# A fused two-block transformer kernel on one core: five changes to the order and the buffers of its stages, the last of them the place of each mLSTM head's step

## What is computed

```python
# first block
n = rmsnorm(h, g_mix);  q_a..z_m = split(n @ w_in)          # 7168 columns
y_a = moba_attention(...)   # 8 heads of 64; y_r = retention(...)  # 4 heads of 128
y_m = memory_attention(q_m, rmsnorm(mem, g_mem), w_mem_kv)  # 4 heads of 128
h = h + (sum of sigmoid(z) * (y @ w_br)) @ w_out
h = h + conv_ffn(rmsnorm(h, g_ffn), w_up, conv_w, conv_b, w_down)   # D_FF = 2816
x = rmsnorm(h, g_final)
# second block, layer 1: mLSTM (4 heads of 256) beside a pooling branch
#   weights of a head: P = (q k^T) * decays;  h = (P v) / max(|sum of P's row|, floor)
#   the head is normed, joined with a skip term and gated by silu(z)
#   pooling branch: windows of 2, 4, 8, 16 tokens, a 256 x 256 matrix for each group
x = x + [ya, yb] @ a_w_out
# second block, layer 2: latent attention (MLA), 8 heads, causal by blocks, output gated
x = x + (attention * silu(z)) @ c_w_out
```

## Time and profile before

| | |
|---|---|
| median of 3 runs | 833.51 us (832.02 to 834.57) |
| the profiled execution | 831.42 us, of which the span from the first to the last instruction is 829.6 us |
| PE busy | 801.0 us, 97% of the span |
| DVE busy | 567.7 us, 68% |
| ACT busy | 432.3 us, 52% |
| POOL busy | 131.4 us, 16% |
| mean granted clock of PE | 0.988 of full |

### The profile page before, as it was taken

One profiled execution on the slowest core, in us unless ns is written; L12 is line 12 of the kernel. 1 busy time (PEld: TensorE's weight loads), 2 busy tenths in 40 slices (PEclk: granted clock), 3 DMA queues, 4 the chain that ended last, 5 costly groups with the idle time before them and its releaser, 6 DMA issues.

```text
span 829.6 us, 11993 instructions
## 1 busy us (share of the span) xinstructions
PE 801.0 (97%) x4640; PEld 698.8 (84%) x4640; DVE 567.7 (68%) x938; ACT 432.3 (52%) x585; POOL 131.4 (16%) x98
## 2 busy tenths in 40 slices
PE   8799999999999999999999999999999989998998
PEld 7588788888888899999988888998898868876766
DVE  5555566796468677878764495769864895896763
ACT  5745544344534475655643464645745245795441
POOL 0011650000000005454440000041410000042000
PEclk9899999999999999999999999999999999998999
DMA  9887433325455465554545544334655333743101
GB/s 342 323 286 258 152 124 134 142 109 172 145 191 203 168 245 192 200 171 186 196 162 201 202 153 170 135 127 167 231 183 190 107 109 115 283 162 143 51 1 51
DMA packets 23220, 142.78 MB, mean 172 GB/s; under 512 B 3548, under 2 KB 4456, under 8 KB 7040
## 3 DMA queue, kind: packets, MB, share of 16 engines
q1 hardware_dynamic: 20016, 134.51, 45.2%
q10 hardware_dynamic: 1776, 4.12, 1.3%
q0 software_dynamic: 1376, 3.43, 1.2%
HBM read 140.97 MB, written 2.64 MB: 173 GB/s over the span
## 4 chain that ended last, share of the span: by engine, by line
PE 77%; DVE 14%; ACT 4%; issue 2%; DMA 2%; SPq 0%; ACTq 0%; DVEq 0%
PE gemm L471 15%; PE gemm L472 15%; PE gemm L473 15%; PE gemm L477 8%; PE gemm L478 8%; PE gemm L479 8%; DVE wlo L1646 4%; DMA raw<-in_weights 2%; ACT whi L1148 2%; DVE xc L2165 2%; PE head L537 1%; PE head L727 1%; PE head L872 1%; PE head L871 1%; DVE rs_a L1656 1%
## 5 line engine op out<-in xcount | busy, mean ns | idle before, releaser
L1646 DVE TENSOR_TENSOR wlo<-raw,whi 128x2048 fp32r<-128x2048 f32 x122 | 282.1, 2314 | 119.9 <-ACT whi L1148 119.7
L1148 ACT CAST whi<-raw 128x2048 fp32r<-128x2048 f32 x122 | 232.6, 1906 | 216.9 <-PE gemm L473 122.3
L471 PE MATMUL gemm<-whi,x0hi 128*128 128x512 f32 (+2 forms) x400 | 158.7, 397 | 4.3 <-DVE x0lo L1833 2.6
L473 PE MATMUL gemm<-whi,x0lo 128*128 128x512 f32 (+2 forms) x400 | 154.9, 387 | 0.0
L472 PE MATMUL gemm<-wlo,x0hi 128*128 128x512 f32 (+2 forms) x400 | 154.9, 387 | 0.0
L477 PE MATMUL gemm<-x1hi,whi 128*128 128x256 f32 x400 | 114.5, 286 | 3.4 <-DVE om L2208 2.7
L478 PE MATMUL gemm<-x1lo,whi 128*128 128x256 f32 x400 | 113.8, 285 | 0.0
L479 PE MATMUL gemm<-x1hi,wlo 128*128 128x256 f32 x400 | 113.8, 284 | 0.0
L471 PEld LDWEIGHTS gemm<-whi,x0hi 128*128 128x128 f32 x400 | 76.0, 190 | 20.8 <-DVE x0lo L1833 3.3
L473 PEld LDWEIGHTS gemm<-whi,x0lo 128*128 128x128 f32 x400 | 75.9, 190 | 15.1
L472 PEld LDWEIGHTS gemm<-wlo,x0hi 128*128 128x128 f32 x400 | 76.1, 190 | 13.7
(11 more groups left out here) (345 smaller groups left out, 1356.4 us busy)
## 6 DMA issues: line engine op xcount, KB each, us to landing
raw<-in_weights SPq DMA_DIRECT2D x122, 1024.0 KB, 4.8
raw<-in_weights SPq DMA_DIRECT2D x4, 512.0 KB, 6.4
bias_rows<-bias_row POOLq DMA_DIRECT2D x1, 1536.0 KB, 15.0
memt<-in_memt SPq DMA_DIRECT2D x4, 256.0 KB, 5.3
tok<-in_mem SPq DMA_DIRECT2D x1, 1024.0 KB, 9.6
xt<-in_xt SPq DMA_DIRECT2D x1, 1024.0 KB, 12.2
xres<-in_x ACTq DMA_DIRECT2D x1, 1024.0 KB, 7.8
bias<-bias_rows POOLq DMA_DIRECT2D x8, 128.0 KB, 4.3
```

The lines of the kernel that those rows point to most:

```text
L471: mm(o, xh, wh, start=start, stop=False)
L473: return mm(o, xl, wh, start=False, stop=stop)
L1148: nc.scalar.copy(whi[:, p % RING, :], raw[:, p % RING, :]).then_inc(s_hi, 1)
L1646: V.tensor_tensor(wlo[:, p % RING, :], raw[:, p % RING, :], whi[:, p % RING, :].bitcast(F32), ALU.subtract).then_inc(s_lo, 1)
```

## The change

Five edits, in the order of the pieces:

1. *Opening order.* The memory tokens are queued after the first half of piece 1, then piece 3 ahead of `xt`, which comes in two halves with pieces 4 and 5 between and behind them; ACT asks for `xres` one step later.
2. *Four banks.* Groups 2 and 3 of `pool`, `wq` and `wk` use the other two banks, and wait for the chunk four back. In step 83 (`pool`) ACT and DVE split piece 85 after the pooled mix is split, not before.
3. *Ones column.* `v_ml` has 257 columns a head, the last one ones (a memset on POOL, behind the `zm` pieces and ahead of POOL's scaling of `xc`); the row sums come out of the weighing product, one token tile in `A[3]`, the other in `A[0]`.
4. *Odd steps.* In the MLA tail DVE subtracts pieces 118 to 123 at the ends of the odd steps 1, 3, ... 11, each one step ahead of its use; ACT copies `pe_q` ahead of the exponentials.
5. *mLSTM step first.* DVE runs `ml_dve` ahead of the subtraction of the piece, not behind it; `ya_lo` stays behind both.

```diff
-LATE_SPLIT = (p0("up"), p0("xp") - 1, p0("xp"), p0("xp") + 1, p0("cu") - 1, p0("cu"), p0("cu") + 1)
+LATE_SPLIT = (p0("pool"), p0("up"), p0("xp") - 1, p0("xp"), p0("xp") + 1, p0("cu") - 1, p0("cu"), p0("cu") + 1)
-            [("u_up", [P, 2, 2, S], F32)], [("v_ml", [P, T, D], F32)])
+            [("u_up", [P, 2, 2, S], F32)], [("v_ml", [P, T, ML_H, S + 1], F32)])
+        FOUR = [c0(name) + n for name in ("pool", "wq", "wk") for n in (2, 3)]
         def bank(c, t=0):
-            return G[2 * (c % 2) + t]
+            return G[2 * (c % 2) + (1 if c in FOUR else t)]
+        def ml_bank(t):
+            return A[3] if t == 0 else A[0]
...
-            sp.wait_ge(s_piece[0], 16)
+            def next_piece(p):
+                sp.wait_ge(s_lo, p - RING + 1)
+                sp.dma_start(raw[:, p % RING, :], ins["weights"][p]).then_inc(s_piece[p % RING], 16)
+            sp.wait_ge(s_half_piece[1], 16)
             sp.dma_start(tok[:, 12:14, :, :].rearrange("p a b c -> p (a b c)"), ins["mem"]).then_inc(s_mem, 16)
-            sp.dma_start(xt[:, :, :].rearrange("p k s -> p (k s)"), ins["xt"]).then_inc(s_xt, 16)
+            next_piece(3)
+            sp.dma_start(xt[:, 0:4, :].rearrange("p k s -> p (k s)"), ins["xt"][:, 0:4 * S]).then_inc(s_xt[0], 16)
+            next_piece(4)
+            sp.dma_start(xt[:, 4:8, :].rearrange("p k s -> p (k s)"), ins["xt"][:, 4 * S:8 * S]).then_inc(s_xt[1], 16)
+            next_piece(5)
             sp.dma_start(ident[:, :], ins["ident"]).then_inc(s_ident, 16)
-            with sp.Fori(1, rounds) as r:
+            with sp.Fori(2, rounds) as r:
@@ ml_weigh @@
                     for i, st in enumerate(range(t + 1)):
                         col = t * P if st == 0 else S
-                        mm(A[3][:, t * S:t * S + S], prob[:, h % 2, col:col + P],
-                           v_ml[:, st, h * S:h * S + S], start=i == 0, stop=st == t)
-                for t in range(T):
-                    for i, st in enumerate(range(t + 1)):
-                        col = t * P if st == 0 else S
-                        last = mm(A[0][:, 400 + t:401 + t], prob[:, h % 2, col:col + P], ones[:, 0:1],
-                                  start=i == 0, stop=st == t)
+                        last = mm(ml_bank(t)[:, 0:S + 1], prob[:, h % 2, col:col + P],
+                                  v_ml[:, st, h, :], start=i == 0, stop=st == t)
@@ PE, pool / wq / wk @@
-                        chunk_free(pe, c - 2)
+                        chunk_free(pe, c - (2 if g < 2 and name != "wk" else 4))
@@ ACT, MLA tail @@
+                    if e < 2:
+                        for k in (2 * e, 2 * e + 1):
+                            act.wait_ge(s_lpt, k + 1)
+                            nc.scalar.copy(pe_q[:, k, :], A[3 - k % 2][:, :]).then_inc(s_ltp, 1)
                     if 1 <= e < MLA_H + 1:
                         h = e - 1
...
-                if p == 1:
+                if p == 2:
                     act.dma_start(xres[:, :, :].rearrange("p t d -> p (t d)"), ins["x"]).then_inc(s_x, 16)
@@ ACT and DVE, behind the pooled mix @@
+                if p == p0("pool"):
+                    split(p + 2)
@@ DVE, ml_dve @@
-                    V.scalar_tensor_tensor(hm[h % 2], om[:, :, h * S:h * S + S], 1.0,
-                                           A[3][:, :].rearrange("p (t d) -> p t d", t=T),
-                                           ALU.add, ALU.mult).then_inc(s_hm, 1)
+                    for t in range(T):
+                        i = V.scalar_tensor_tensor(hm[h % 2][:, t, :], om[:, t, h * S:h * S + S], 1.0,
+                                                   ml_bank(t)[:, 0:S], ALU.add, ALU.mult)
+                    i.then_inc(s_hm, 1)
...
-                    order(V.tensor_copy(rsum[:, :], A[0][:, 400:402]))
+                    for t in range(T):
+                        i = V.tensor_copy(rsum[:, t:t + 1], ml_bank(t)[:, S:S + 1])
+                    order(i)
@@ DVE, MLA tail @@
-                split(Z0 + 2)
                 for e in range(14):
...
-                    if e % 2 == 0:
-                        split(piece_of(e) + 2)
+                    if e % 2:
+                        split(piece_of(e + 1))
@@ DVE, main loop @@
                 head_dve(p)
+                ml_dve(p)
                 if p not in LATE_SPLIT:
                     split(p + 2)
-                ml_dve(p)
                 if p < ML0 + 6:
                     ya_lo(p)
@@ POOL @@
+            pool.wait_ge(s_mm, p0("zm") + 4)
+            Q.memset(v_ml[:, :, :, S:S + 1], 1.0).then_inc(s_vones, 1)
             pool.wait_ge(s_xclo, 4)
```

More of the change, by code:

```diff
@@ L286, in program @@
         s_memt = [s_memt] + [sem(f"mem_columns_loaded_{i}") for i in range(2, 5)]
+        s_xt = [s_xt, sem("x_columns_loaded_2")]
         s_gain, s_onehot = sem("gains_loaded"), sem("onehot_loaded")
@@ L322, in program @@
         s_hm = sem("ml_h_gated")
+        s_vones = sem("value_ones_ready")
         s_md = sem("max_rows_moved")
@@ L806, in ml_step @@
                 if e == 0:
+                    pe.wait_ge(s_vones, 1)
                     pe.wait_ge(s_gcol, 1)
@@ L1250, in input_hi @@
                     else:
-                        act.wait_ge(s_xt, 16)
+                        act.wait_ge(s_xt[i // 2], 16)
                     for kb in (2 * i, 2 * i + 1):
@@ L1436, in mla_tail @@
                         z_tanh((e - 2) // 4)
-                    if e < 2:
-                        for k in (2 * e, 2 * e + 1):
-                            act.wait_ge(s_lpt, k + 1)
-                            nc.scalar.copy(pe_q[:, k, :], A[3 - k % 2][:, :]).then_inc(s_ltp, 1)
                     k_scale(e + 2)
@@ L1518, in empty @@
                         for t in range(T):
-                            done = nc.scalar.copy(v_ml[:, t, n * 512:n * 512 + 512], bank(c, t)[:, :])
+                            done = nc.scalar.copy(v_ml[:, t, 2 * n:2 * n + 2, 0:S],
+                                                  bank(c, t)[:, :].rearrange("p (h d) -> p h d", d=S))
                     elif name in ("wq", "wk"):
@@ L2205, in empty @@
                     elif name == "pool":
+                        dve.wait_ge(s_zd, n + 1)
                         for b in range(2):
```

## The result

The changed kernel takes 820.6 us (median of 4 runs, 817.46 to 821.15), the kernel before 832.76 us (4 runs beside it). The ratio is 0.9847, its 95% interval 0.9825 to 0.987: 12.2 us faster, where 12.3 had been forecast, and 821.2 us stands against 820.6. The profiled execution took 820.15 us with a span of 818.4: 11.3 less than the profiled one of before, so term by term the sum can only be held against some 11.3 us, one less than forecast.

What follows compares the result with a forecast made beforehand. PE, busy 97% of an 829.6 us span, bounds the kernel. Opening -2.8, `pool` -2.1, `wq` -0.6, ones column and mLSTM order +0.8, MLA tail -7.6 sum to -12.3: median 833.5 to 821.2 us, range 816.5 to 825.2.

Steps and rivals of the forecast that it cites:

- keeps its half clock: Opening: PE's wait for `x0lo` before piece 4 grows to nearly 4 us, with the half clock behind it as before.
- So a wait of 2.4 and up costs its length: All PE waits: 2.4 us and up also costs half the slow stretch behind, 1.7 for 3.4 us, 3.3 for 6.5.
- which I price without half clock, by the wait at 800.9: Pooling, piece 84: new wait of 2.1 us, full clock assumed behind it; gain 2.1, or 0.4 with half clock.
- three steps at 0.3 more: mLSTM steps on DVE: split gating and a second copy add 0.3 us a head, 0.9 in three, 0.8 taken.
- if piece 104 starts earlier after the first score than now: mLSTM steps: a sign that the forecast is wrong, since piece 104 was to start later, 0.8 us lost.
- A second slow stretch, in piece 103, would hide: mLSTM steps: more half clock in piece 103 would vanish in the 4 us that PE then waits.
- less the 1.0 that the copies now take in front: MLA tail start: exponentials come 4.4 us earlier without two subtractions, less 1.0 for `pe_q` copies ahead of them.
- ready near 757.4, while PE asks at 758.6: MLA tail start: exponentials done before PE needs them, so the 2.7 us wait and 3.3 of half clock go.
- The mLSTM order pays: Rival, mLSTM steps: the `xc` wait and its half clock go, 7.4 us gained instead of 0.8 lost, 813.0; chance 0.06.
- Half clock comes back: Rival: two more slow stretches, behind piece 84's new wait and in tail or mLSTM steps, +3.4 us, 824.6; chance 0.17.
- The opening gives nothing: Rival, opening: piece 3 lands no earlier despite the new load order, 824.0 us; chance 0.09.
- late raw loads in the tail: Rival, MLA tail: late subtractions delay loads of pieces 121 to 123, so PE waits, 836.2 us; chance 0.02.

Runs made afterwards that it cites:

- open_back: Kernel after with the old load order of the opening (tokens, both `xt` halves and identity ahead of piece 3, `xres` a step earlier): 822.62 us, ratio 0.9881 to before.
- order_alone: Kernel before with only the mLSTM step moved ahead of the subtraction, `ya_lo` still behind both: 834.1 us, ratio 1.0033 to before.
- banks_back: Kernel after with two banks again for the groups of `pool`, `wq` and `wk`, piece 85's subtraction left in its new place: 822.96 us, ratio 0.9892 to before.
- yalo_first: Kernel after with `ya_lo` between the mLSTM step and the subtraction: 816.81 us, ratio 0.9809 to before.
- fill2: Kernel after with ten unneeded products of ones on PE before the turn of the last mLSTM head: 818.32 us, ratio 0.9836 to before.
- ml_back: Kernel after with the mLSTM step put back behind the subtraction, the other four edits kept: 818.66 us, ratio 0.9832 to before.
- tail_sub_back: Kernel after with DVE's MLA tail subtractions back before the loop and on even steps, `pe_q` copies still ahead of the exponentials: 825.08 us, ratio 0.9903 to before.

## Why the prediction was right

**The opening.** Its mechanism and its first number held: 2.65 against 2.8, and `open_back` gives it back. The statement that PE's longer wait "keeps its half clock" was too kind: the stretch was 6.8 us and not 3.4 in this profile, which took back 1.26. In the eleven traces in which a wait of 4.2 stands there uncovered, the stretch is 6.8 in six and 3.4 in five (6.8 also in `order_alone`, where the opening is the old one). Up to FFN down, the traces with the new opening and this wait gained 1.2 to 2.6 on that of before: this is what the term is worth.

**The rule on the clock.** "So a wait of 2.4 and up costs its length" and half of a slow stretch was drawn from one execution, and does not hold as it stands. In `order_alone` and `open_back` a wait of 2.4 and 2.5 before piece 3 left the clock at full; waits of 2.0 to 2.2, below the bound, brought half clock in 9 cases of 21. Behind all 20 waits of 2.6 and more that PE stood out without other work it did fall.

**Four banks.** The new wait before piece 84, its length (2.02 against 2.1) and its cause held: with the subtraction behind the emptying it is gone. The step "which I price without half clock, by the wait at 800.9" was luck. Of nine traces with this wait of 2.0 six have a slow stretch behind it and three do not. At `wq` and `wk` the term was too small: from the end of the second wait for `wlo` in `om` to the first score 1.15 were gained, not 0.6, and `banks_back` gives as much back. Shorter waits before the other groups, under 0.3 each, go as well. Another 0.4 came from shorter waits for `wlo` in `om`, which I had left as they were; they differ by as much between traces of equal code (0.47 and 0.87 in the two of the kernel after), so that is no gain of the change.

**Ones column and mLSTM order.** The forecast was that the order does not pay because the same work stands before the last `x1lo`, and that the wait moves there from `xc`. Both are seen in the earlier trace rows against the rows of after, and `order_alone` and `yalo_first` show it from both sides. The start of this stretch of DVE's work was right too: 17.70 after S, against 17.71 before and 18.99 in `order_alone`, where PE still computes the row sums ahead of the score. The total (0.8 lost, 0.89 measured) agrees, but by two errors that cancel, which is luck. The term "three steps at 0.3 more" was mis-sized: a gating half costs 0.33 from start to start (the row of 0.476 that it was taken from is another operation's) and the second copy 0.06, so a step grew by about 0.1. Nor is it so that DVE did not pause in the kernel before: it did for 0.41 and 0.53, and one such pause, of 0.46, is left. So piece 104 starts 46.19 after the first score instead of 46.30: 0.1 earlier, which by the prediction's own sign ("if piece 104 starts earlier after the first score than now") counts against it. And "A second slow stretch, in piece 103, would hide" came true in `fill2` and `banks_back`, but what counted in the kernel after was another place: the stretch behind the waits before piece 104 grew from 3.4 to 6.8, on the path, 1.0 us. Split by runs: from S to C the ones column alone gains 0.9 (`ml_back`). The order costs 1.1 by itself (`order_alone`), and beside the ones column 0.7 where the slow stretch is 3.4 as in `ml_back`, 1.8 where it is 6.8. For POOL's scaling of `xc` "nothing" was right: of its eight operations the two beside a subtraction took 3.53 and 2.58 us where the others took 0.92 to 1.04, and the subtractions took 2.29 as elsewhere. Where the two engines met, POOL's operation was held up and not DVE's.

**The tail.** 6.94 from C to the end against a forecast of 7.6. That the first wait goes with its half clock (2.43 and 3.1), and the one for `olo` (2.07), held, and so did the new wait at the end (0.37, with what follows 0.65, against 0.5). The step "less the 1.0 that the copies now take in front" was mis-sized: it left out the table load of 1.28, which the copies push out of ACT's wait, so the exponentials start 1.9 after the maxima and the 1.2 us of slack forecast ("ready near 757.4, while PE asks at 758.6") became a wait of 0.3. And the sum put all 2.7 on DVE's subtractions: `tail_sub_back` shows that with DVE late the copies' place alone takes 1.0 off the wait, and in this one trace the half clock with it.

**The rivals.** "The mLSTM order pays" is out by `order_alone`. "Half clock comes back" is in part true in every execution, in other places than I had named each time, and goes with the scatter of 817.5 to 821.2: the shortest runs of the kernel after have the highest mean granted clock, 0.994, the longest 0.989 to 0.991. "The opening gives nothing" is out. Of late raw loads in the tail there is no trace: PE waits for no split there but the last.

**The sum.** In the traces the opening gave 1.4 less than forecast, the four banks and what follows them up to the first score 1.1 more, the mLSTM steps 0.1 less, the tail 0.7 less: 11.25 in all against 12.3. That the medians stand 12.2 apart is closer than the terms are. The mechanisms held; half clock, which the sum fixed for each place, differs from execution to execution by more than 1 us. The "seven releasers, 19.5 us in all" are those that the edits touch: four more waits of 1.0 to 1.3 us (for `relb`, `cqlo`, `v_c` and `u_up`) stand in the trace of before and of after alike.

## What to carry to other kernels

A wait names the last signal, and moving that signal forward is worth nothing when another one from the same busy engine stands right behind it: count the work ahead of *both* signals in the old and the new order. Where an engine has slack over a whole region but PE waits in it, what matters is which of its jobs is ahead of PE's next need; a subtraction that is used a step later belongs behind every product that is used now. What stands in a wait unseen, like ACT's table load, comes on the path when other work is moved ahead of it. And price half clock behind a wait as a chance, from several executions, not from one.

## What the runs showed of the hardware

- The granted clock behind the same wait differs between executions of the same code. Behind the wait of 2.0 us before piece 84, six traces of nine show 3.4 us at half clock (6.8 in none), three show full clock; behind the wait of 4.2 before piece 4 it is 6.8 in six traces and 3.4 in five. Behind the wait of 2.2 before piece 103 it is 3.4 in two traces of nine, behind the waits of 2.4 and 2.5 before piece 3 in one of three, behind the five of 2.6 to 2.7 always. Behind a wait of 1.7 (`tail_sub_back`) it stayed at full.
- Two waits of 1.2 and 2.2 us with 0.6 us of work between them brought 6.8 us at half clock in five traces of eight, and 3.4 in the other three; one wait of 3.3 to 3.6 brought 3.4 (the kernel before, `ml_back`) or 6.8 (`yalo_first`, `banks_back`). A stretch can begin inside the wait (at 673.72 in the kernel after, where PE waits until 675.06), and that part of it costs nothing.
- Ten or twelve products of 128 x 128 ones in a wait, 0.24 us each, kept the clock at full behind it in all four cases tried.
- A weighing product of 257 columns costs what one of 256 does (379 and 378 ns), and two DVE operations of 128 x 256 back to back cost 0.06 us more than one of 128 x 512 (from start to start 0.66 against 0.60).
- POOL's operations on `xc` took 0.92 to 1.04 us by themselves and 2.5 to 3.5 beside a subtraction of DVE (before: 2.87, 2.50, 2.73; after: 3.53, 2.58); four of the five subtractions took 2.29, one 2.44.
- ACT's table load ahead of the exponentials takes 1.28 us, in every trace; it costs nothing where ACT waits anyway.
